# The last head group's norms summed in two rounded parts, and a second output tile ahead of the last input pair

## What is computed

```python
def head_norm_gate(o, w, gate):
    """Per-head RMSNorm of o (B,L,H,d) with gain w (d,), times swish(gate)."""
    y = o * lax.rsqrt(jnp.mean(o * o, axis=-1, keepdims=True) + EPS) * w.astype(jnp.float32)
    ...
merged = (jax.nn.sigmoid(ga.astype(jnp.float32)) * o_gla
          + jax.nn.sigmoid(gb.astype(jnp.float32)) * o_hg).astype(h.dtype)
return merged @ w_out_l, s_gla_new, s_hg_new
```

## Time and profile before

| what | value |
|---|---|
| time, median of 3 runs | 1044.99 us (1044.52 to 1045.64) |
| the profiled execution's own time | 1045.55 us |
| its span in the profile | 1043.8 us |
| PE busy | 1032.0 us, 99% of the span |
| weight loads of PE | 961.0 us, 92% |
| DVE busy | 686.6 us, 66% |
| ACT busy | 490.6 us, 47% |
| POOL busy | 64.4 us, 6% |
| granted clock of PE, mean | 0.999 |

### The profile page before, as it was taken

One profiled execution on the slowest core, in us unless ns is written; L12 is line 12 of the kernel. 1 busy time (PEld: TensorE's weight loads), 2 busy tenths in 40 slices (PEclk: granted clock), 3 DMA queues, 4 the chain that ended last, 5 costly groups with the idle time before them and its releaser, 6 DMA issues.

```text
span 1043.8 us, 23604 instructions
## 1 busy us (share of the span) xinstructions
PE 1032.0 (99%) x10226; PEld 961.0 (92%) x10226; DVE 686.6 (66%) x1038; ACT 490.6 (47%) x774; POOL 64.4 (6%) x86
## 2 busy tenths in 40 slices
PE   7999999999999999999999999999999999999998
PEld 7989999989999899999899878999999999888886
DVE  6365745675726767356766578988888888744544
ACT  5433454632736335545327557644444444633532
POOL 6100003100003000031000000000000000000000
PEclk9999999999999999999999999999999999999999
DMA  7523224623227222345222291142332332422212
GB/s 197 166 78 83 62 72 117 188 62 82 72 63 221 81 66 62 92 119 166 75 71 91 77 303 37 41 122 81 103 100 82 104 99 62 142 82 84 87 51 91
DMA packets 130775, 105.21 MB, mean 101 GB/s; under 512 B 4272, under 2 KB 115888, under 8 KB 130672
## 3 DMA queue, kind: packets, MB, share of 16 engines
q1 hardware_dynamic: 125520, 85.61, 28.7%
q0 software_dynamic: 4864, 17.83, 5.6%
q10 hardware_dynamic: 288, 0.27, 0.1%
HBM read 91.89 MB, written 11.80 MB: 99 GB/s over the span
## 4 chain that ended last, share of the span: by engine, by line
PE 93%; DVE 2%; ACT 2%; DMA 1%; DVEq 0%; ACTq 0%; issue 0%
PE ps L294 34%; PE ps L2056 23%; PE ps L2080 12%; PE ps L1279 10%; PE ps L1212 2%; PE ps L1187 1%; PE ps L1202 1%; PE ps L414 1%; PE ps L1214 1%; PE ps L1219 1%; DMA w_raw_t<-in_w_out_dram 1%; PE ps L1171 1%; PE ps L1135 1%; PE ps L1251 1%; PE ps L1183 1%; PE ps L2091 1%
## 5 line engine op out<-in xcount | busy, mean ns | idle before, releaser
L280 ACT ACTIVATE w_hi_t<-w_raw_t 128x1024 fp32r<-128x1024 f32 x73 | 77.2, 1057 | 256.5 <-PE ps L294 173.8
L294 PE MATMUL ps<-x_hi,w_lo_t 128*128 128x288 f32 x880 | 192.3, 300 | 0.0
L294 PE MATMUL ps<-x_hi,w_hi_t 128*128 128x288 f32 x880 | 188.2, 295 | 0.0
L294 PE MATMUL ps<-x_lo,w_hi_t 128*128 128x288 f32 x880 | 187.8, 295 | 0.0
L284 DVE TENSOR_TENSOR w_lo_t<-w_raw_t,w_hi_t 128x1024 fp32r<-128x1024 f32 x73 | 89.1, 1220 | 133.0 <-ACT w_hi_t L280 131.9
L294 PEld LDWEIGHTS ps<-x_hi,w_lo_t 128*128 128x128 f32 x880 | 140.7, 188 | 4.4 <-issue 2.5
L294 PEld LDWEIGHTS ps<-x_lo,w_hi_t 128*128 128x128 f32 x880 | 141.5, 188 | 0.0
L294 PEld LDWEIGHTS ps<-x_hi,w_hi_t 128*128 128x128 f32 x880 | 141.4, 188 | 0.0
L2056 PE MATMUL ps<-x_hi,w_lo_t 128*128 128x288 f32 x276 | 81.5, 295 | 0.0
L2056 PE MATMUL ps<-x_lo,w_hi_t 128*128 128x288 f32 x276 | 81.3, 295 | 0.0
L2056 PE MATMUL ps<-x_hi,w_hi_t 128*128 128x288 f32 x276 | 81.3, 295 | 0.0
(11 more groups left out here) (383 smaller groups left out, 2336.1 us busy)
## 6 DMA issues: line engine op xcount, KB each, us to landing
w_raw_t<-in_w_in_dram SPq DMA_DIRECT2D x57, 512.0 KB, 3.8
merged<-in_w_ffn_in_dram SPq DMA_DIRECT2D x22, 512.0 KB, 5.3
w_raw_t<-in_w_ffn_in_dram SPq DMA_DIRECT2D x22, 512.0 KB, 4.6
w_raw_t<-in_w_ffn_out_dram SPq DMA_DIRECT2D x22, 512.0 KB, 3.7
w_raw_t<-in_w_in_dram SPq DMA_DIRECT2D x32, 256.0 KB, 3.9
h_t<-in_x_prompt_dram SPq DMA_DIRECT2D x8, 512.0 KB, 6.7
h_t<-in_state_gla_dram POOLq DMA_DIRECT2D x4, 1024.0 KB, 6.1
h_t<-in_state_hgrn_dram POOLq DMA_DIRECT2D x8, 512.0 KB, 8.2
```

The costliest lines, as they stand in the source:

```text
L280: nc.scalar.activation(w_hi_t[:, u % NSPL, 0:nk, :], w_raw_t[:, u % NRAW, 0:nk, :], ACT.Copy).then_inc(w_hi, 1)
L294: m = nc.tensor.matmul(out[:, q, :], w[:, u % NSPL, k, :], x(k, q), start=first and i == 0, stop=last and i == len(todo) - 1)
```

## The change

Group 3 now sums its squares as the other groups do. `in_parts` is gone. For the two HGRN heads ACT makes two more copies (576 columns each) to a rounded form in `QT_round`, a second name for the tile `QT`; the first waits for ss1's matmuls, which read what lay there. POOL makes the rests, and for the GLA head both parts. PE's norm matmuls are twelve `fp32r` ones in the place of six float32 ones. ACT makes `out_hi(UB+5)` behind the norms, no longer ahead of them; DVE makes `out_lo(UB+5)` one multiplication later. PE multiplies units UB+4 and UB+5 with token tile 1 ahead of UB+3, no longer behind it.

```diff
-            if in_parts(j):
-                pool.wait_ge(sq_hi, j + 1)
-                for h in (1, 2):
-                    nc.gpsimd.tensor_tensor(square_part(j, h, False), norm_rows(j)[h - 1], square_part(j, h, True).bitcast(F32),
-                                            ALU.subtract).then_inc(sq_lo, 1)
+            pool.wait_ge(sq_hi, j + 1)
+            for h in (1, 2):
+                nc.gpsimd.tensor_tensor(square_part(j, h, False), norm_rows(j)[h - 1], square_part(j, h, True).bitcast(F32),
+                                        ALU.subtract).then_inc(sq_lo, 1)
...
-            if d0 == 2 and in_parts(j):
+            if d0 == 2:
+                if j == G - 1:
+                    act.wait_ge(step_done, NO[j, "ss1"] + 1)
                 for h in (1, 2):
                     ins = act.activation(square_part(j, h, True), norm_rows(j)[h - 1], ACT.Copy)
                 ins.then_inc(sq_hi, 1)
...
         out_hi(act, UB + 4)
-        out_hi(act, UB + 5)
         norm(G - 1, (1, 2))
         norm(G - 1, (0,))
+        out_hi(act, UB + 5)
...
         gated(G - 1, 2)
-        out_lo(dve, UB + 5)
         dve.wait_ge(rst, (G - 1) * 3 + 2)
         dve.tensor_tensor(O[:, 2:4, :], O[:, 2:4, :], rs_two(G - 1), ALU.mult)
+        out_lo(dve, UB + 5)
...
-        pe.wait_ge(w_lo, UB + 5)
+        pe.wait_ge(step_free[1], USES[1] + 1)
+        for u in (UB + 4, UB + 5):
+            for kk in range(2):
+                out_part(nc.tensor, u, 1, kk, u == UB + 4 and kk == 0, kk == 1)
         for kk in range(2):
             pe.wait_ge(m_lo, KT - 1 + kk)
...
-        pe.wait_ge(step_free[1], USES[1] + 1)
         pe.wait_ge(w_lo, UB + 8)
-        for u, c in ((UB + 6, 0), (UB + 4, 1), (UB + 5, 1), (UB + 6, 1)):
+        for u, c in ((UB + 6, 0), (UB + 6, 1)):
```

More of the change, by code:

```diff
@@ L308, in build @@
     O = A("O", [P, 4, T])
+    QT_at = nc.sbuf_base
     QT = A("QT", [P, 2, 3, T])
@@ L380, in rs_two @@
         return T3[:, 0:2, :] if j == G - 1 else k_flat[:, 0:2 * T].rearrange("p (a t) -> p a t", a=2)
-    def in_parts(j):
-        return j < G - 1
     def square_part(j, h, hi):
@@ L387, in square_part @@
             return E2_round[:, 1 if hi else 0, :]
+        if j == G - 1:
+            return QT_round[:, 1 if hi else 0, h - 1, :]
         return K_round[:, h, :] if hi else k_t_round[:, h - 1, :]
     def summed(j):
-        return 3 * (j + 1) if in_parts(j) else 3 * (G - 1) + 1
+        return 3 * (j + 1)
     def out_w(u, hi):
@@ L427, in second @@
         return ap.rearrange("p (n b) -> p n b", b=2 * L)[:, :, L:2 * L]
+    QT_round = nc.alloc_sbuf_tensor_at("QT_round", [P, 2, 3, T], F32R, offset=QT_at)
     E2_round = nc.alloc_sbuf_tensor_at("E2_round", [P, 2, T], F32R, offset=E2_at)
@@ L553, in add_squares @@
             nc.gpsimd.tensor_tensor(E2[:, 0, :], E2[:, 0, :], E2[:, 1, :], ALU.add).then_inc(sq_sum, 1)
[L554 to L559, removed]
+            pool.wait_ge(sq_sum, summed(j) - 2)
+            nc.gpsimd.tensor_copy(square_part(j, 0, True), E2[:, 0, :]).then_inc(sq_sum, 1)
+            pool.wait_ge(sq_sum, summed(j) - 1)
+            nc.gpsimd.tensor_tensor(square_part(j, 0, False), E2[:, 0, :], square_part(j, 0, True).bitcast(F32),
+                                    ALU.subtract).then_inc(sq_sum, 1)
         pool.wait_ge(x_hi_s, NX)
@@ L1227, in do_step @@
                     pe.wait_ge(sq_sum, summed(j))
-                elif in_parts(j):
+                else:
                     pe.wait_ge(sq_hi, j + 1)
                     pe.wait_ge(sq_lo, j * 2 + h)
-                else:
-                    pe.wait_ge(o_sq, j * 4 + (2, 3, 4)[h])
                 if j == 0 and h == 0:
@@ L1236, in do_step @@
                     half = slice(q * HT, (q + 1) * HT)
[L1237 to L1241, removed]
+                    for hi in (False, True):
+                        m = nc.tensor.matmul(s[:, q * 512:q * 512 + HT], ones_r[:, :], square_part(j, h, hi)[:, half], start=not hi, stop=hi)
             elif name in ("ss0", "ss2"):
@@ L2007, in _ @@
                     ins.then_inc(out_done, 1)
-        pe.wait_ge(step_free[1], USES[1] + 1)
         pe.wait_ge(w_lo, UB + 8)
-        for u, c in ((UB + 6, 0), (UB + 4, 1), (UB + 5, 1), (UB + 6, 1)):
+        for u, c in ((UB + 6, 0), (UB + 6, 1)):
             for kk in range(2):
-                out_part(nc.tensor, u, c, kk, u == UB + 4 and kk == 0, kk == 1)
+                out_part(nc.tensor, u, c, kk, False, kk == 1)
         pe.wait_ge(w_lo, UB + 9)
```

## The result

The changed kernel takes 1049.88 us (1049.08 to 1050.85, 6 runs), the kernel before 1045.08 us (1044.52 to 1046.13, 6 runs) beside it: a ratio of 1.0048, 95% interval 1.0038 to 1.0058. The direction was forecast; the time lies 0.6 us above the end of the range. The profiled execution took 1049.55 us, its span is 1047.8 us, its mean granted clock 0.998.

What follows compares the result with a forecast made beforehand. The end of UB+3, which starts an ACT/DVE chain, was taken to bound the feed-forward layer's start. UB+3's later end, 1.75, plus norm1's delay, 0.95, gave +2.7 us: 1047.7 us, range 1046.0 to 1049.3.

Steps and rivals of the forecast that it cites:

- UB+3's end sets the feed-forward layer: Feed-forward layer starts when UB+3's last tile lets ACT go: PE arrives at 641.4, the ACT/DVE chain at 641.67.
- Rival B: The ACT/DVE chain before the feed-forward layer has unseen slack, so PE's own work decides: -1.05 us, 1043.9; chance 0.12.
- rival A: DVE's unbroken stream keeps POOL out until the state updates, so norm1's start stays: +1.75 us, 1046.7; chance 0.33.
- rival C: Second tile doesn't fill PE's wait for the input pair, only 0.1 us before; already in the sum, no own chance.
- Work moved ahead of UB+3, 1.75 us: UB+4 and UB+5 with tile 1, 2.80 us, run ahead of UB+3, which ends 1.75 us later even if norm1's start stays.
- N, 0.95 us: N is when PE starts norm1; POOL delays DVE by 1.8 us, less 0.86 of room, so it moves 0.95 us.
- the first stretch: DVE's unbroken work from 589.52 to 592.70, where POOL's cast and first subtraction get in between and cost DVE 1.8 us.
- a draw of 0.02 us that I give to DVE: POOL's next subtraction pair (597.32) against DVE's product (597.34): DVE taken to go first, costing nothing rather than 1.27 us.
- The end of +2.2: Both POOL subtractions behind 597.32 win too, norm1 starts 2.2 us later; a third of the forecast's 0.52.
- The clock, at nothing in the sum and a chance of 0.03: Something larger, such as a fall of the granted clock behind PE's new 3 us wait at the turns; chance 0.03.
- upper case: Both subtractions behind 597.32 win over DVE's product: +1.75+2.2 = +4.0 us, 1049.0.
- ACT's two copies at nothing: Two added copies in front of UB+3's split, 0.69 us or less each, end far ahead of DVE's product; cost nothing.

Runs made afterwards that it cites:

- the second tile alone: Kernel before with only PE's new order: UB+4 and UB+5 with token tile 1 ahead of UB+3. 1048.71 us, ratio 1.0036.
- the norms in parts: Kernel before with only the last group's norms in rounded squares and rests, engine order as before. 1048.80 us, ratio 1.0039; profiled once more, 1049.90 us.
- PE's old order: Changed kernel with UB+4 and UB+5 with tile 1 back behind UB+3. 1048.42 us, ratio 1.0034.

## What of the prediction was right, and which step failed

- **UB+3's end sets the feed-forward layer: right.** Forecast from the earlier trace rows, shown by the chain column. Rival B, slack in the chain, is refuted, and so is rival A (N moved in all eight profiles with POOL's work in that place); rival C's point, that the wait for the pair was only 0.1 us, is confirmed by the run with the second tile alone. Of the product's shift, 5.31 us where the sum gives 2.7, the excess is 1.31 us in N, 0.14 in the moved work and 1.16 behind UB+3.
- **Work moved ahead of UB+3, 1.75 us: right.** Measured 1.89 and 1.79 us with the clock up. The inner steps: four matmuls per norm step 0.133 us apart (eight in 1.32 us), 0.54 us of wait in front of UB+5 where 0.75 was forecast, none in front of UB+3, none in front of UB+7. (The gains listed there add up to 1.1 us, not 1.05; the 1.75 comes from the timeline and doesn't use them.)
- **N, 0.95 us: the step that failed.** The mechanism and its prices were right (1.8 us for the first stretch, 1.72 measured; 1.27 for one subtraction, 1.33 measured), and N moved by 2.26 us. What failed is the sentence "the second is a draw of 0.02 us that I give to DVE". POOL took it in all eight profiles. The end of +2.2, which the prediction gave a third of the forecast's own chance, is what N did. By the prediction's own rows POOL was ready 0.02 us ahead of DVE (597.32 and 597.34), so it had no reason to take the cheaper side, all the less as the same text had POOL getting in ahead of DVE in the first stretch.
- **The clock, at nothing in the sum and a chance of 0.03: the second step that failed.** The prediction forecast the wait of "some 3 us" and then gave a fall of the clock behind it almost no chance, on the mean clock of 0.999, a mean over a kernel that had no such wait. Behind 2.80 to 2.93 us it fell in five profiles out of five; behind 2.74 us in one it did not. In the profile of the changed kernel the first product comes 1.16 us late behind UB+3, and 1.12 of it are gone with the clock held up. In the medians that run differs by 0.3 us only, within the spread, so what the fall costs in the time is not shown.
- 1.75 + 2.2 alone, the end listed, is the 1049.0 that the prediction named as its upper case; the remaining 0.9 us to 1049.88 is of the size of the clock's part in the trace, and that it is the clock is argued, not shown. The range ended at 1049.3, so the subtraction given to DVE alone would have left the time inside it.
- **ACT's two copies at nothing: right.** N is back with them in place when POOL's work is moved, and ACT stood idle for 7.68 us behind its last split, until norm1 let its first Ln go:

```profile
606.12 1.37 ACT L689 ACTIVATE QT<-ps,eps_c 128x576 f32<-128x576 f32 x2 [7.68 <-PE ps L1237]
```

## What to carry to other kernels

Ahead of filling a wait, measure it at that very place: 2.80 us of work were put where 0.1 us of waiting stood (some 1.9 with the norms changed, an estimate), in front of the unit that a chain on two other engines starts from. Work put on POOL cost nothing here only beside DVE instructions that take one large operand from SBUF; look for that place and not for POOL's idle time. Behind a new wait of PE of nearly 3 us the clock fell in five profiles of six, so where such a wait can't be removed, allow for a stretch at half rate behind it.

## What the runs showed of the hardware

**POOL and DVE excluded each other by whole instructions**, and took turns in all but one case. With both queues full, a DVE instruction on two SBUF operands and a POOL instruction each waited for the whole of the other's: 0.47 us behind a cast of 0.66, 1.25 behind a subtraction of 1.42, 1.33 and 2.71 (4.06 less 1.35) behind one and two of them. The Trainium skill, SBUF — State Buffer, section Who interferes with whom, states the exclusive use and the full block; the trace agrees, save that 0.07 to 0.19 us of each overlap was not lost. That POOL is let in first when both are ready within 0.02 us, and that it may be let in twice, stands on these eight profiles alone; why is open.

**The clock fell behind waits of 2.80 to 2.93 us**, to the lower level of 1.2 GHz, and not behind one of 2.74 in one profile. It also fell behind shorter ones: behind 1.55 and 1.68 us with 1.3 us of matmuls between them in the second profile of the norms in parts, and behind 1.55 and 0.30 us in the profile with PE's old order (0.55 in the stretch from 608 to 610 us). Five other profiles had these last waits too, some 1.5 us and then 0.3, and no fall there. So the same waits brought a fall in one execution and none in another, and what decides it is open.
